# Gate rows and evictions ahead of the sums' splits, one output-weight tile per half step, the weight tile first in each step's transfers

## The chip, the cores and the metric

One Trainium2 chip, one core of it. A core has TensorE (PE, the matrix engine, with a granted clock of 1.2 or 2.4 GHz), VectorE (DVE), ScalarE (ACT), GpSimd (POOL) and SyncE (SP, which here only issues transfers). Each runs its own instructions in program order; semaphores hold them together. The metric is device time of one execution in microseconds (us); lower is better.

## The reference

One layer of a hybrid encoder trunk on x of 1024 tokens by 1024 features, all float32. What matters here:

```python
h = rmsnorm(x, norm1_g)
z = h @ w_in + b_in                     # 1024 x 2312
aq, ak, av, mq, mk, mv, mo, mi, mf = split(z)
att = window_sink_attention(aq, ak, av, sinks)        # 16 chunks of 64 tokens
ml = sigmoid(mo) * mlstm_chunkwise(conv_silu(mq, mk), mv, mi, mf)
#   log_f = log_sigmoid(mf); cum_f = cumsum(log_f)    # the gate rows
x = x + concat(rmsnorm(att), rmsnorm(ml)) @ w_out
x = x + conv_ffn(rmsnorm(x))
return rmsnorm(x, final_g)
```

## The kernel before

Each float32 product is done as three passes over operands that are split in a high part (rounded, written by ACT) and a low part (the rest, written by DVE): high*high, high*low, low*high. So every weight tile and every activation passes through ACT and then DVE before PE can use it.

The work around the change is the first projection, z = h @ w_in, and what is woven into it:

- **Blocks.** `z_block(b)` computes one tile of 128 columns of z for all tokens, 48 matmuls of 128x512. Blocks 0 to 3 (0 is the gates' 8 columns) are done as the input arrives; blocks 4 to 10 follow, two PSUM buffers taking turns. Block b waits for the low part of its own weights (`z_split`, from `weight_low(b)`) and for the eviction of the block two before it (`z_scaled`, from `z_scale`, which multiplies the PSUM result by each token's 1/rms). `z_keep` on ACT then adds the bias.
- **Gate rows.** Block 0's eight rows become the mLSTM's decay rows: `gate_logs` (ACT: abs, exp, log, with two table loads), `gate_rows(0)` and `gate_rows(1)` (DVE: two scans and some elementwise work on 4 partitions), `gate_exps` (ACT). They are turned by PE between blocks 6 and 7.
- **Sums.** Part of z (columns MO and MV, the `wide_unit` calls after block 10) is computed by a scheme with seven half-size products (`WIDE_ORDER`) instead of eight. It needs sums and differences of slices of h, made on POOL (`add_sums(kk)`, four of 128x512 for each of four kk, in the order `SUM_TURN`), split by `sums_high` (ACT) and `sums_low` (DVE), stored to DRAM by `store_sums` (SP) and loaded back later (`load_sums`). It also needs sums of weights, made on POOL by `add_weights(p, q)` from the tiles that `load_quarters` and the `w_t3` loads bring.
- **Output weights.** The eight row tiles of w_out are loaded (`load_wo`), split (`wo_high` on ACT, `wo_low` on DVE) and stored (`store_wo`), at half steps given by the table `WO_AT`, in four places of SBUF given by `WO_PLACE`, a place being loaded again when `WO_FREED` says that its content is stored.
- **Attention.** From block 8 on, chunk n of the attention runs in half steps beside the blocks: `att_step(b+1, half)` gives n. In each, DVE does `att_top(n)`, ACT `att_exps(n)`, DVE `att_sum(n)`, POOL `att_p_scale(n)`, PE turns and attends.
- **The order on each engine is written out by hand.** ACT and DVE run a loop over blocks b and halves, each with a fixed list of calls; POOL a loop over chunks n with the tables `weight_sums` and `DECAY_KEEPS`; SP a loop over n, the number of the weight tile, whose body lists the transfers of that step in the order in which they are issued. SP stops at each wait, and all transfers behind it stop too.

In the profile, L2350 is the blocks' matmuls, L1595 and L1600 are `z_scale`, L1561 `weight_low`, L1810 `sums_low`, L1633 to L1651 the gate rows, L1155 `sums_high`, L1146 `sum_scale`, L1011 `weight_high`, L1742 and L1125 the output weights' split, L925 to L931 `add_sums`, L949 `add_weights`, L2584 to L2588 the wide units. At the end of the stage, `ml_key` (L1139) scales the turned keys for PE's `ml_state` (L2485), and `wide_gate` (L1130) is the sigmoid of the output gate.

## Time and profile before

| | us |
|---|---|
| median of 3 runs | 1010.95 (1010.78 to 1011.40) |
| the profiled execution's own time | 1012.26 |
| its span, first to last instruction | 1010.5 |
| PE busy in it | 981.3 (97%) |
| DVE, ACT, POOL busy | 763.8, 527.9, 96.4 |
| mean granted TensorE clock | 0.991 of 2.4 GHz |

The table is read from the first part of the page: PE is busy for all but 29.2 us of the span, and no other engine for more than 76% of it. The list of waits and the chain that ended last say where the 29.2 us are.

### The profile page before, as it was taken

The page shows a single profiled execution, that of the slowest core. Times are in us where ns is not written, and L with a number is a line of the kernel's source. Part 1 is how long each engine was busy: PE and PEld are TensorE (multiplying, and loading weights), DVE is VectorE, ACT ScalarE, POOL GpSimd, SP SyncE. Part 2 cuts the span into 40 slices and gives each one's busy share as a digit, 9 for nine tenths or more (in the row PEclk, how much of TensorE's full clock was granted, in tenths as well). Part 3 has the DMA queues.
Part 4 walks back from the last instruction along what each step waited for, and adds up shares of the span by engine and source line. Part 5 has one row for each costly group of instructions (what it writes and reads, how often), then busy time and mean ns, then how long its engine had stood idle before and what let it go on. Part 6 is the DMA issues. An engine that isn't in the chain of part 4 may idle for free.

```text
span 1010.5 us, 12942 instructions
## 1 busy us (share of the span) xinstructions
PE 981.3 (97%) x4665; PEld 802.7 (79%) x4665; DVE 763.8 (76%) x1166; ACT 527.9 (52%) x1020; POOL 96.4 (10%) x77
## 2 busy tenths in 40 slices
PE   8968989999999999999999999999999999999997
PEld 6746877787788888888888888888888888888886
DVE  4377577887755668997777777877776879995796
ACT  4875454667853326654544544544543634444574
POOL 2380133342310000000000000000000000000000
PEclk9998999999999999999999999999999999999999
DMA  9465968717622242333223223223322999035104
GB/s 340 166 229 193 395 225 289 256 58 228 211 84 84 84 146 63 113 97 111 77 70 99 82 65 100 87 63 96 92 63 84 392 350 359 1 113 190 42 1 166
DMA packets 101239, 150.67 MB, mean 149 GB/s; under 512 B 6572, under 2 KB 56876, under 8 KB 100152
## 3 DMA queue, kind: packets, MB, share of 16 engines
q1 hardware_dynamic: 100360, 149.24, 43.6%
q8 instruction: 37, 0.61, 0.2%
q10 hardware_dynamic: 720, 0.61, 0.2%
q0 software_dynamic: 96, 0.00, 0.1%
q14 instruction: 26, 0.21, 0.1%
HBM read 112.62 MB, written 36.74 MB: 148 GB/s over the span
## 4 chain that ended last, share of the span: by engine, by line
PE 85%; DVE 5%; DMA 3%; ACT 3%; SPq 2%; POOL 1%; issue 1%; DVEq 0%; ACTq 0%
PE pz L2653 8%; PE pz L2654 8%; PE pz L2655 8%; PE pd L2653 6%; PE pd L2654 6%; PE pd L2655 6%; PE pz L2350 5%; PE pd L2679 4%; PE pd L2678 4%; PE pd L2676 4%; PE pz L2679 3%; PE pz L2678 3%; PE pz L2676 3%; PE pd L2544 3%; PE pd L2546 3%; PE pd L2545 3%
## 5 line engine op out<-in xcount | busy, mean ns | idle before, releaser
L1349 ACT ACTIVATE ws_hi<-raw 128x512 fp32r<-128x512 f32 x88 | 52.9, 626 | 102.8 <-PE pz L2655 47.3
L2653 PE MATMUL pz<-ht_hi,ws_hi 128*128 128x512 f32 x240 | 93.5, 390 | 0.0
L2655 PE MATMUL pz<-ht_hi,ws_lo 128*128 128x512 f32 x240 | 93.4, 389 | 0.0
L2654 PE MATMUL pz<-ht_lo,ws_hi 128*128 128x512 f32 x240 | 93.4, 389 | 0.0
L2653 PE MATMUL pd<-ht_hi,ws_hi 128*128 128x512 f32 x200 | 77.9, 390 | 0.0
L2655 PE MATMUL pd<-ht_hi,ws_lo 128*128 128x512 f32 x200 | 77.8, 389 | 0.0
L2654 PE MATMUL pd<-ht_lo,ws_hi 128*128 128x512 f32 x200 | 77.8, 389 | 0.0
L2097 DVE SCALAR_TENSOR_TENSOR gate<-u,vec,gate 128x1023 f32<-128x1023 f32 (+1 forms) x44 | 56.5, 1283 | 19.4 <-ACT gate L1391 18.6
L2067 DVE TENSOR_TENSOR ws_lo<-raw,ws_hi 128x512 fp32r<-128x512 f32 x88 | 58.5, 686 | 0.7 <-ACT ws_hi L1349 0.7
L2097 DVE SCALAR_TENSOR_TENSOR lift<-u,vec,lift 128x1023 f32<-128x1023 f32 (+1 forms) x44 | 56.2, 1278 | 0.1
L1424 ACT ACTIVATE d_hi<-a 128x512 fp32r<-128x512 f32 x44 | 27.8, 631 | 54.2 <-PE pd L2679 26.3
L2653 PEld LDWEIGHTS pz<-ht_hi,ws_hi 128*128 128x128 f32 x240 | 45.0, 188 | 10.0 <-issue 0.7
L2655 PEld LDWEIGHTS pz<-ht_hi,ws_lo 128*128 128x128 f32 x240 | 45.0, 188 | 9.5
L2654 PEld LDWEIGHTS pz<-ht_lo,ws_hi 128*128 128x128 f32 x240 | 45.0, 188 | 9.2
L2584 PE MATMUL pz<-w_hi,h_hi 128*128 128x512 f32 x112 | 45.8, 409 | 5.9 <-DVE z L1600 2.6
L2676 PE MATMUL pz<-d_hi,d_hi 128*128 128x512 f32 x132 | 51.4, 389 | 0.0
L2678 PE MATMUL pz<-d_lo,d_hi 128*128 128x512 f32 x132 | 51.4, 389 | 0.0
L2679 PE MATMUL pz<-d_hi,d_lo 128*128 128x512 f32 x132 | 51.4, 389 | 0.0
L2678 PE MATMUL pd<-d_lo,d_hi 128*128 128x512 f32 x132 | 51.3, 389 | 0.0
L2679 PE MATMUL pd<-d_hi,d_lo 128*128 128x512 f32 x132 | 51.3, 389 | 0.0
L2676 PE MATMUL pd<-d_hi,d_hi 128*128 128x512 f32 x132 | 51.3, 389 | 0.0
L2544 PE MATMUL pd<-wo_hi,mix_hi 128*128 128x512 f32 x128 | 50.7, 396 | 0.0
(339 smaller groups left out, 2602.8 us busy)
## 6 DMA issues: line engine op xcount, KB each, us to landing
raw<-in_w_up SPq DMA_DIRECT2D x48, 512.0 KB, 5.1
b<-in_w_down SPq DMA_DIRECT2D x49, 256.0 KB, 7.1
act_rows<-gate SPq DMA_DIRECT2D x22, 512.0 KB, 2.6
a<-act_rows SPq DMA_DIRECT2D x44, 256.0 KB, 4.7
x_in<-in_x SPq DMA_DIRECT2D x8, 512.0 KB, 12.1
s_hi_rows<-s_hi SPq DMA_DIRECT2D x4, 1024.0 KB, 3.9
s_lo_rows<-s_lo SPq DMA_DIRECT2D x4, 1024.0 KB, 6.9
wo_hi_rows<-wo_new_hi SPq DMA_DIRECT2D x8, 512.0 KB, 4.3
```

The costliest lines, as they stand in the source:

```text
L1349: nc.scalar.activation(ws_hi[m][:, :, :], summand(p, i), ACT.Copy).then_inc(s["ws_hi_made"], 1)
L2067: nc.vector.tensor_tensor(ws_lo[m][:, :, :], summand(p, i), ws_hi[m][:, :, :].bitcast(F32), ALU.subtract)\
L2097: nc.vector.scalar_tensor_tensor(out=dst[:, back:], in0=src[:, 0:S - back], scalar=w, in1=dst[:, back:], op0=ALU.mult, op1=ALU.add).then_i ...
L2350: ins = mm(dst[:, h * HALF:(h + 1) * HALF], w[:, c], h_part(part, k, h), start=first, stop=last)
L2544: mm(bank[4 + n % 4], mix_hi[u][:, k, :], wo_hi[:, k, c], start=k == 0, stop=False)
L2584: mm(wide_bank(t), h_hi[:, k, tok], hi[:, kk, :], start=begins and q + kk == 0, stop=False, skip_group_check=not begins)
L2653: mm(dst, wh[:, k, :], xh[:, k, :], start=begins and k == 0, stop=False, skip_group_check=not begins)
L2654: mm(dst, wh[:, k, :], xl[:, k, :], start=False, stop=False, skip_group_check=not begins)
L2655: ins = mm(dst, wl[:, k, :], xh[:, k, :], start=False, stop=k == KH - 1, skip_group_check=not begins)
L2676: mm(dst, d_hi[m, 0][:, c], d_hi[m, 1][:, :], start=begins and k == 0, stop=False, skip_group_check=not begins)
L2678: mm(dst, d_hi[m, 0][:, c], d_lo[m, 1][:, :], start=False, stop=False, skip_group_check=not begins)
L2679: ins = mm(dst, d_lo[m, 0][:, c], d_hi[m, 1][:, :], start=False, stop=k == KT - 1, skip_group_check=not begins)
```

## The change

Nothing is computed otherwise; instructions and transfers change their places. On PE the order is the same, word for word.

1. **ACT**: `gate_logs` right behind `z_keep(0)`, ahead of `sums_high(1)`; `sums_high(2)` behind `sum_scale(3)`; `sums_high(0)` behind `weight_high(6)`.
2. **DVE**: `z_scale(1)`, `z_scale(2)`, `z_scale(3)` and `gate_rows(0)` ahead of all `sums_low`; these stand at the second half of b = 3 (kk 1), 4 (kk 2) and 5 (kk 0 and 3). In the wide units `weight_low` stands behind `att_keep`.
3. **WO_AT**: at most one output-weight tile in each half step, from (6, 0) to (10, 0) instead of from (5, 0) to (9, 1). The last tile takes another place.
4. **SP**: the weight tile first in each step, the sums' stores and output-weight transfers behind it; `load_quarters` a step later; `load_sums(5)` and the bias rows ahead of the last output-weight store and of the `w_t3` loads; `spread_decay` a step later.
5. **POOL**: the weight sums one or two chunks later; the decay's masks (`DECAY_KEEPS`) and ACT's exponentials (`DECAYS`) one chunk later at first.
6. **ACT, end of the stage**: `ml_key(1)` ahead of four `wide_gate`.

```diff
-DECAYS = {12: (0,), 13: (1,), 14: (2,), 15: (3, 4), 16: (5, 6, 7)}
-DECAY_KEEPS = {11: (0,), 12: (1, 2), 13: (3, 4), 14: (5, 6), 15: (7,)}
+DECAYS = {13: (0,), 14: (1, 2), 15: (3, 4), 16: (5, 6, 7)}
+DECAY_KEEPS = {12: (0,), 13: (1, 2), 14: (3, 4), 15: (5, 6, 7)}
-WO_AT = {(5, 0): 0, (5, 1): 1, (6, 1): 2, (7, 0): 3, (7, 1): 4, (8, 1): 5, (9, 0): 6, (9, 1): 7}
+WO_AT = {(6, 0): 0, (6, 1): 1, (7, 0): 2, (7, 1): 3, (8, 0): 4, (8, 1): 5, (9, 0): 6, (10, 0): 7}
-WO_PLACE = (0, 1, 2, 3, 0, 1, 3, 0)
-WO_FREED = {4: 0, 5: 1, 6: 3, 7: 4}
+WO_PLACE = (0, 1, 2, 3, 0, 1, 3, 1)
+WO_FREED = {4: 0, 5: 1, 6: 3, 7: 5}
...
             def load_quarters():
                 sp.wait_ge(*sum_stored[3])
+                sp.wait_ge(wo_stored[0], 32 * 2)
...
-            store_sums(1)
-            store_sums(2)
             for n in range(7, LAST_BLOCK + 1 + UNITS):
                 if n in LOADED:
                     load_tile(n)
                 if n == 7:
-                    load_wo(0)
-                    load_wo(1)
-                    store_sums(0)
+                    store_sums(1)
                 if n == 8:
                     store_rows()
+                    load_wo(0)
+                    store_sums(2)
+                    store_sums(0)
+                if n == 9:
+                    load_wo(1)
+                    store_sums(3)
                     load_wo(2)
                     store_wo(0)
+                if n == 10:
                     load_wo(3)
                     store_wo(1)
...
                 if n == 13:
                     sp.wait_ge(s["z_done"], LAST_BLOCK + 1)
                     load_sums(5)
...
+                    store_wo(7)
+                    sp.wait_ge(wo_stored[0], 32 * (NK // 2))
+                    for q in range(2):
+                        sp.dma_start(w_t3[q][:, :], w_wide[0, 2 + q]).then_inc(b22_loaded, 16)
...
-            weight_sums = {2: (5, 0), 3: (5, 1), 6: (6, 0), 7: (6, 1), 8: (7, 0), 9: (7, 1)}
+            weight_sums = {4: (5, 0), 5: (5, 1), 7: (6, 0), 8: (6, 1), 9: (7, 0), 10: (7, 1)}
...
-            sums_high(1)
-            z_keep(0)
-            sums_high(2)
-            gate_logs()
+            z_keep(0)
+            gate_logs()
+            sums_high(1)
             sum_scale(3)
-            sums_high(0)
+            sums_high(2)
...
             att_total_keep()
+            ml_key(1)
             for i in range(NT // 2, NT):
                 wide_gate(i)
...
             z_scale(0)
-            sums_low(1)
             z_scale(1)
             z_scale(2)
-            sums_low(2)
...
-                    if (b, half) in ((3, 1), (5, 0)):
-                        sums_low(0 if b == 3 else 3)
+                    if half == 1 and b in (3, 4, 5):
+                        for kk in {3: (1,), 4: (2,), 5: (0, 3)}[b]:
+                            sums_low(kk)
```

DVE before, from block 0's eviction to that of block 4 (`s_lo_277` to `s_lo_280` are the sums' low parts, `zq` and `z` the evictions, `row_*` the gate rows, `w_lo_268` the low part of block 6's weights):

```order
L1810 TENSOR_TENSOR s_lo_278<-s_sum_274,s_hi_282 128x2048
L1595 TENSOR_TENSOR zq<-pz,rstd_row 128x8x64 x2
L1595 TENSOR_TENSOR zq<-pd,rstd_row 128x8x64 x2
L1810 TENSOR_TENSOR s_lo_279<-s_sum_275,s_hi_283 128x2048
L1595 TENSOR_TENSOR zq<-pd,rstd_row 128x8x64 x2
L1633 SCALAR_TENSOR_TENSOR row_b<-row_b,row_c 4x1024
L1636 SCALAR_TENSOR_TENSOR row_d<-reset,row_b 4x1024
L1637 COPY row_b<-row_d 4x1024
L1639 TENSOR_TENSOR row_a<-row_a,row_b 4x1024
L1640 COPY row_c<-row_b 4x7
L1810 TENSOR_TENSOR s_lo_277<-s_sum_273,s_hi_281 128x2048
L1561 TENSOR_TENSOR w_lo_268<-w_raw_265,w_hi_271 128x1024
```

The same place of DVE with the change (its lines are numbered some higher):

```order
L1599 TENSOR_TENSOR zq<-pz,rstd_row 128x8x64 x2
L1599 TENSOR_TENSOR zq<-pd,rstd_row 128x8x64 x4
L1637 SCALAR_TENSOR_TENSOR row_b<-row_b,row_c 4x1024
L1640 SCALAR_TENSOR_TENSOR row_d<-reset,row_b 4x1024
L1641 COPY row_b<-row_d 4x1024
L1643 TENSOR_TENSOR row_a<-row_a,row_b 4x1024
L1644 COPY row_c<-row_b 4x7
L1814 TENSOR_TENSOR s_lo_278<-s_sum_274,s_hi_282 128x2048
L1565 TENSOR_TENSOR w_lo_268<-w_raw_265,w_hi_271 128x1024
```

Two of the three low parts that stood ahead of block 6's weights are behind them now, and the gate rows' first half has nothing of the sums ahead of it.

ACT before, from the last scaled sum to the gates' logarithm (`s_hi_282` and `s_hi_283` are the high parts of kk 1 and 2):

```order
L1155 ACTIVATE s_hi_282<-s_sum_274 128x2048
L1040 ACTIVATE row_a<-row_d,gate_b 4x1024
L1042 ACTIVATE row_b<-row_d,gate_b 4x1024
L1155 ACTIVATE s_hi_283<-s_sum_275 128x2048
L1053 ACTIVATE row_c<-row_b 4x1024
L1055 ACT_TABLE_LOAD
L1055 ACTIVATE row_c<-row_c 4x1024
L1057 ACT_TABLE_LOAD
L1057 ACTIVATE row_c<-row_c,one 4x1024
```

ACT with the change, the same place:

```order
L1041 ACTIVATE row_a<-row_d,gate_b 4x1024
L1043 ACTIVATE row_b<-row_d,gate_b 4x1024
L1054 ACTIVATE row_c<-row_b 4x1024
L1056 ACT_TABLE_LOAD
L1056 ACTIVATE row_c<-row_c 4x1024
L1058 ACT_TABLE_LOAD
L1058 ACTIVATE row_c<-row_c,one 4x1024
L1156 ACTIVATE s_hi_282<-s_sum_274 128x2048
```

Both high parts, each of which waits for POOL's sums, are behind the logarithm now.

SP before, the transfers around the end of block 10 (`w_t_0_291`, `w_t_1_292` are the `w_t3` tiles):

```order
L619 DMA wo_hi_rows<-wo_new_hi_61 128x1024
L619 DMA wo_lo_rows<-wo_new_lo_57 128x1024
L681 DMA w_t_0_291<-in_w_wide 128x1024
L681 DMA w_t_1_292<-in_w_wide 128x1024
L594 DMA h_hi<-s_hi_rows 128x4x512
L594 DMA h_lo<-s_lo_rows 128x4x512
L687 DMA bias_rows<-in_b_in 128x512 x2
```

SP with the change:

```order
L595 DMA h_hi<-s_hi_rows 128x4x512
L595 DMA h_lo<-s_lo_rows 128x4x512
L684 DMA bias_rows<-in_b_in 128x512 x2
L620 DMA wo_hi_rows<-wo_new_hi_62 128x1024
L620 DMA wo_lo_rows<-wo_new_lo_58 128x1024
L689 DMA w_t_0_291<-in_w_wide 128x1024
L689 DMA w_t_1_292<-in_w_wide 128x1024
```

The bias rows no longer stand behind the last output-weight store and the two weight tiles.

## Rows read from the trace of the kernel before

**Rows 1.** The page: length of the profiled execution.
```profile
span 1010.5 us, 12942 instructions
```
**Rows 2.** Waits of PE: who waited for whom, us in total, times, longest.
```profile
PE pz L2350 <- DVE zq L1595: 13.1, 2, 12.2
PE pz L2584 <- DVE z L1600: 2.6, 1, 2.6
PE pz L2584 <- DVE ml_v L1782: 1.6, 1, 1.6
PE pd L2485 <- ACT ml_k L1139: 1.2, 1, 1.2
PE pd L2413 <- ACT probs_t L1111: 0.7, 1, 0.7
```
**Rows 3.** Timeline of PE, 79 us: start, us, instruction, in brackets idle before it.
```profile
79.38 1.19 PE L2350 MATMUL pz<-h_hi,w_hi 128*128 128x512 f32 x2 [12.17 <-DVE zq L1595]
```
**Rows 4.** The chain that ended last, blocks 6 and 7: start, us.
```profile
79.38 13.71 PE pz L2350 x48
...
94.74 11.11 PE pz L2350 x48
```
**Rows 5.** Timeline of DVE, 54 to 83 us.
```profile
54.61 1.29 DVE L1595 TENSOR_TENSOR zq<-pz,rstd_row 128x512 f32<-128x512 f32 x2
...
64.99 1.22 DVE L1633 SCALAR_TENSOR_TENSOR row_b<-row_b,row_c 4x1024 f32<-4x1024 f32 x1 [1.93 <-ACT row_c L1057]
...
68.55 1.58 DVE L1637 COPY row_b<-row_d 4x1024 f32<-4x1024 f32 x1
70.17 2.18 DVE L1639 TENSOR_TENSOR row_a<-row_a,row_b 4x1024 f32<-4x1024 f32 x1
...
73.54 2.29 DVE L1810 TENSOR_TENSOR s_lo<-s_sum,s_hi 128x2048 fp32r<-128x2048 f32 x1
75.75 2.28 DVE L1561 TENSOR_TENSOR w_lo<-w_raw,w_hi 128x1024 fp32r<-128x1024 f32 x1
...
81.66 1.21 DVE L1647 TENSOR_TENSOR row_c<-m_prev,row_d 4x1024 f32<-4x1024 f32 x1
```
**Rows 6.** Timeline of POOL, 49 to 56 us.
```profile
49.76 1.30 POOL L925 TENSOR_TENSOR s_sum<-s_sum 128x512 f32<-128x512 f32 x1
...
52.51 3.20 POOL L929 TENSOR_TENSOR s_sum<-s_sum 128x512 f32<-128x512 f32 x1
```
**Rows 7.** Timeline of ACT, 45 to 60 us.
```profile
45.30 1.14 ACT L1146 ACTIVATE s_sum<-x_turned,vec 128x1024 f32<-128x1024 f32 x1
...
51.66 1.13 ACT L1040 ACTIVATE row_a<-row_d,gate_b 4x1024 f32<-4x1024 f32 x1
...
59.06 1.06 ACT L1053 ACTIVATE row_c<-row_b 4x1024 f32<-4x1024 f32 x1
```
**Rows 8.** Busy time by window, each engine; then granted clock, DMA share, GB/s.
```profile
79.38:82.00 2.62, 2.62 (x6) 2.12 (x7) 2.55 (x3) 2.32 (x2) 0.00 (x0) 0.50 1.03 338
...
152.30:157.00 4.70, 4.70 (x15) 3.70 (x16) 2.47 (x4) 1.84 (x6) 1.99 (x1) 0.64 0.97 320
```
**Rows 9.** Timeline of DVE, 131 us.
```profile
131.27 3.42 DVE L1668 SCALAR_TENSOR_TENSOR qk_acc<-z,vec,qk_acc 128x1022 f32<-128x1022 f32 x1
```
**Rows 10.** The chain that ended last, 140 to 165 us.
```profile
140.27 2.54 DVE wo_new_lo L1742
...
154.07 10.15 DMA bias_rows<-in_b_in
```
**Rows 11.** The page, transfers: KB each, median us to landing.
```profile
s_lo_rows<-s_lo SPq DMA_DIRECT2D x4, 1024.0 KB, 6.9
```
**Rows 12.** Timeline of ACT, 254 to 261 us.
```profile
254.34 2.17 ACT L1130 ACTIVATE ml_gate<-ml_gate 128x512 f32<-128x512 f32 x4
...
258.03 0.91 ACT L1139 ACTIVATE ml_k<-pd,decay 128x64 f32<-128x64 f32 x4
260.06 0.93 ACT L1139 ACTIVATE ml_k<-pd,decay 128x64 f32<-128x64 f32 x4 [1.12 <-PE pd L2473]
```

More of the change, by code:

```diff
@@ L648, in _ @@
                 if n == 7:
-                    load_wo(0)
-                    load_wo(1)
-                    store_sums(0)
+                    store_sums(1)
                 if n == 8:
                     store_rows()
+                    load_wo(0)
[4 more added lines that the diff above has]
+                    store_sums(3)
                     load_wo(2)
                     store_wo(0)
+                if n == 10:
                     load_wo(3)
                     store_wo(1)
-                if n == 9:
-                    store_sums(3)
+                    load_wo(4)
                     store_wo(2)
-                    load_wo(4)
-                if n == 10:
-                    store_wo(3)
-                    load_wo(5)
-                    load_quarters()
-                    store_wo(4)
                 if n == 11:
@@ L672, in _ @@
                           .then_inc(s["att_v_moved"], 16)
+                    load_wo(5)
+                    store_wo(3)
                     load_wo(6)
+                    store_wo(4)
+                    load_quarters()
+                if n == 12:
                     store_wo(5)
                     load_wo(7)
-                if n == 12:
                     store_wo(6)
-                    store_wo(7)
-                    sp.wait_ge(wo_stored[0], 32 * (NK // 2))
-                    for q in range(2):
-                        sp.dma_start(w_t3[q][:, :], w_wide[0, 2 + q]).then_inc(b22_loaded, 16)
                 if n == 13:
@@ L694, in _ @@
                     weights_used(sp, 16)
+                    spread_decay()
                     load_sums(7)
-                if n == 18:
-                    spread_decay()
                 if n == 23:
@@ L957, in _ @@
                     add_weights(*weight_sums[n])
+                if n == NC - 1:
+                    add_weights(4, 0)
                 for i in DECAY_KEEPS.get(n, ()):
                     decay_keep(i)
-            add_weights(4, 0)
             add_weights(4, 1)
@@ L1185, in _ @@
                         att_exps(n)
+                    if (b, half) == (4, 0):
+                        sums_high(0)
                     if half == 0 and b <= LAST_BLOCK:
@@ L1257, in _ @@
             for i in range(NT - 1):
-                ml_key(i + 1)
+                if i:
+                    ml_key(i + 1)
                 if i == NT - 3:
@@ L1764, in wide_keep @@
                     dve.wait_ge(s["gates_t_ready"], 1)
-                    dve.wait_ge(wo_stored[1], 32 * (NK // 2))
+                    dve.wait_ge(wo_stored[0], 32 * (NK // 2))
                 if m == 24:
@@ L1832, in _ @@
                         weight_low(b + 2)
-                    if 0 <= v < UNITS - 1:
-                        weight_low(LAST_BLOCK + 2 + v)
                     if half == 0 and b < LAST_BLOCK:
@@ L1841, in _ @@
                                 att_keep(m)
+                    if 0 <= v < UNITS - 1:
+                        weight_low(LAST_BLOCK + 2 + v)
                     if 0 <= n < NC:
```

## The prediction

> **What bounds the kernel now.** Read first the list of waits of PE, since PE is busy for nearly the whole span. Two waits of the blocks' matmuls for an eviction make 13.1 us, one of them 12.2; later there are single waits of 2.6, 1.6, 1.2 and 0.7 us [rows 2]. Then PE's timeline: block 6 starts at 79.38 after 12.17 us of idleness, so block 5 had ended at 67.21 [rows 3]; the other wait, 0.9, is block 5's own start. The chain that ended last shows block 6 taking 13.71 us, where block 7 takes 11.11 [rows 4], and the windows show why: from 79.38 to 82.00 the granted clock was 0.50 of 2.4 GHz, that is 1.2 GHz [rows 8].
>
> What held block 6 is on DVE [rows 5]. It needs the low part of its weights (w_lo at 75.75, till 78.03) and the eviction of block 4 (z_scale, till 79.2). Both stand behind the gate rows, which start at 64.99 when ACT's logarithm ends, and behind a sums' low part at 73.54. The gates' logarithm on ACT was late because the gates' bias starts only at 51.66, behind the first high part of the sums, and the abs only at 59.06, behind the second; ACT's last scaled sum had ended at 46.4 [rows 7]. Between them ACT waited for POOL's sums.
>
> **The first stall, walked anew.** ACT: the bias pair follows the scaled sums at 46.4; it takes 2.3 (two instructions, the first 1.13), and from the abs's start to the logarithm's end the trace has 64.95 - 59.06 = 5.9 [rows 5, 7]. So the gate rows start at 46.4 + 2.3 + 5.9 + 0.2 for the hand-overs = 54.8 instead of 65.0. The evictions of blocks 1 to 3 are done by then: three of 1.2 to 1.3 us [rows 5] from 46.5 on.
>
> The gate rows now meet POOL's sums, which run without a break. An add on POOL takes 1.30 alone, and 3.20 when it meets DVE [rows 6]; a copy takes 1.58 and a product of the two row tiles 2.18 on DVE where POOL is busy, against 1.21 for the same form at 81.66 with POOL idle [rows 5]. In the rows the two take strict turns: each waits for the other's instruction to end. The eviction from PSUM at 54.61 took 1.29 though POOL was in its slow add [rows 5, 6], so evictions don't take part.
>
> By the Trainium skill (GPSIMD Engine Reference, section 1, Specifications), GpSimd shares its SBUF interfaces with VectorE and contends with DVE instructions that have two SBUF inputs. The trace agrees, by the 2.18 against 1.21 for a form with two; this speaks against a change that moves such rows into POOL's busiest stretch, and it is priced below from the rows.
>
> With turns, DVE goes: waits 0.4 for POOL, 1.1, scan 2.3 (66.2 to 68.5 in the trace) after 1.1, copy 0.6 after 1.1, subtraction 1.1 after 1.1, the small copy 0.1 after 1.1: the first half of the gate rows ends at 64.9. That is 10.1 us where the trace before has 8.5 (64.99 to 73.5). Then the low part of kk 1, 2.3 (at 73.54) to 67.2; block 6's low weights 2.2 (at 75.75) to 69.4; block 4's eviction 1.2 to 70.6. ACT is ahead: the high part of kk 1 (1.9), the scaled sums of kk 3, the high part of kk 2, three biases and block 6's high weights end at 64.9. Block 6 starts at 70.8 instead of 79.4. Block 5 starts 0.9 earlier, since its bank is free at once, and ends at 66.1. The wait is 4.7 instead of 12.2.
>
> Bounds: without any turns lost to POOL (five of about 1.1) DVE is ready at 67.4 (ACT's high weights, 64.9, then bound the low ones), a wait of 1.3; with POOL first at one place more, and one in the evictions, 73, a wait of 7. I take 4.7, since the turns at 68.55 to 75.75 are the nearest rows.
>
> Clock: it fell to 1.2 GHz after the wait of 12.17 us and cost 13.71 - 11.11 = 2.6 us. It fell also after the wait of 2.6 us, where a window of 4.7 us had 0.64 [rows 8], a loss of 0.36 x 4.7 = 1.7. So after 4.7 us of idleness I expect it to fall and take the middle, 2.1. Block 6 ends at 70.8 + 11.1 + 2.1 = 84.0, before at 93.1: **9.1 us** won.
>
> The Trainium skill (TensorE: Matmul & The Clock Gate, Part 1) says that the throttled clock is the default and activity releases it; the trace agrees at both waits. By the page alone one could also hope for a full clock behind a short wait, which would make the sum 2.1 better; that is the second rival.
>
> **What is late next.** Block 7 starts behind the turning of the gate rows (1.6 us) at 85.6. It needs block 5's eviction, which now has behind it on DVE the second half of the gate rows (about 7.5 with two turns lost), the low part of kk 2 (2.3), the low weights (1.2) and itself (1.2): 70.6 + 12.2 = 82.8, and some 84 if ACT, which must do two exponentials, a table load, the high part of kk 3 and block 7's high weights, is the slower. A margin of 1.5 us, so nothing is charged.
>
> Then the output weights. Their tile 1 is loaded only after the sums of kk 2 are stored (split at about 80.4, a transfer lands 6.9 after its issue [rows 11]: 87.5), behind the stores of kk 0 in SP's row: issued at 88.6, here by about 97. ACT stands in `wo_high(1)` until then, and the high weights of block 9 and the attention's values are queued behind it; PE wants the latter at 102.9 and gets them at about 102.3. This is the thinnest margin of the change (0.6), and cost nothing by my sum; each us that the transfer is later is a us of PE.
>
> **The waits of the attention stage.** The 2.6 us wait and the 0.7 before it come from a late DVE: the tap at 131.27 took 3.42 and the output-weight low part at 140.27 took 2.54, both beside POOL's weight sums [rows 9, 10], where a form of this size with POOL idle takes 1.21 [rows 5], and two output-weight tiles stand in the half steps just ahead of block 10's eviction. The change puts those weight sums one to two chunks later and has one tile fewer there. That frees 2.2 + 1.2 + 1.3 = 4.7 us of DVE ahead of an eviction that was 2.6 late. So 2.6 goes, with the clock's 1.7 behind it, and 0.7: **5.0 us**. The 1.6 us wait [rows 2] is for the bias rows: their transfer starts at 154.07, behind a store and two weight tiles in SP's row, and takes 10.15 [rows 10]. Now it is issued with block 10's end and lands at least 4 us earlier relative to PE: **1.6 us**.
>
> **Edits at nothing.** The weight sums, the quarters (issued at about 120 and needed by POOL at 137), the decay transfers and the later masks have several us of room each. They cost up to 2 if the room is used up. `ml_key(1)` ahead of four sigmoids takes away the wait of 1.2 [rows 2]: it would run some 2 us earlier than 258.03. But the sigmoids, the table load and the root, 3.7 us from 254.34 on, then stand between it and the next `ml_key` (260.06, with 1.12 of idleness ahead of it [rows 12]), which becomes up to 1 us late, and PE waits there: net 0.2, bounds 0 and 1.2. I charge 0.
>
> **The sum.** 9.1 + 5.0 + 1.6 = 15.7. The span goes from 1010.5 [rows 1] to 994.8. What lies around the span was 1.8 us (1012.26 less 1010.5), and this execution stands 1.3 above the median; taken off the median, 1010.95 - 15.7 = 995.2 us. Behind 260 us nothing is touched and PE is bound by itself, so what is won there stays.
>
> **The rivals.**
> *The attention stage keeps its waits.* The first stall shrinks, but POOL's weight sums meet DVE elsewhere, or the output weights' loads come late, so that 4 to 6 us of the second and third term are not seen, or new waits take their place: 995.2 + 5 = 1000. For it: DVE is full there, and PE, with no stalls to wait in, gives it less time. Against: the sums of DVE's work per half step stay below PE's.
> *The first stall nearly goes.* DVE gets through with few turns lost, the wait is 1.3, the clock stays up: 4.7 - 1.3 + 2.1 = 5.5 better, 989.7. But then block 7's eviction is the next late thing and takes back 1 or 2: 991.
> *The transfers stop the queue; slower than before.* SP is one row, and load_wo, store_wo and the sums' stores of 1 MB each wait for one another there. If each of output-weight tiles 1 to 3 comes a whole store (6.9, rows 11) later than ACT stands at it, ACT holds the weights and values of blocks 8 to 10: 3 x 6.9 = 20.7 lost, less 15.7: 1016. It decides from 16 us of such lateness on. Against: before the change PE's list has no wait for an output weight or for what stands behind one [rows 2], with the same eight loads and stores in a like weave. One late transfer costs some us only, which is the first rival.
> *The change doesn't take effect* where the logarithm is late for another reason (the gates' row transfer, or the bias's semaphores): the first term falls to about 4, 1000; it lies with the first rival.
>
> **How the numbers follow.** The forecast's case (993 to 998) 60%; the first rival and its like (998 to 1003) 23%; the second (988 to 993) 12%; the slower side 2%; something between 1003 and 1013, 3%. Two runs of this kernel can be told apart by about 0.2%, 2 us. Faster by more than that 0.95, the same 0.03, slower 0.02. The range that leaves at most 2 in 10 out is 990.5 to 1001.5, which holds the clock's and the turns' bounds and half of the first rival.
>
> **What would show it.** PE's wait before block 6 near 4.7 us, between 66 and 71; gate rows starting on DVE at 54.8, with copy and subtraction again at 1.6 and 2.2; a granted clock of 0.5 behind it; block 7 from about 85.6 without a wait; no wait of wide units for block 10's eviction nor for ml_v; PE's first matmul of the output projection some 16 us before the old one. Wrong would be: gate rows later than 57; a wait of PE for the attention's values or for ACT's high weights of block 9; new waits of more than 1 us between 100 and 250.

## The result, and the profile after

The changed kernel takes 1002.79 us (median; 1002.39 to 1003.63, 4 runs), the kernel before 1010.98 (1010.78 to 1011.4, 4 runs): ratio 0.992, with a 95% interval of 0.9902 to 0.9937. That is 8.2 us less, where 15.7 were forecast, and 1.3 us above the forecast range. Its profiled execution has a span of 1000.7 us, 9.8 less than before's [rows 1]; before's profiled run stood 1.3 above its own median and this one 0.3 below its own, so the two numbers agree.

The waits of PE in the changed kernel (who waited for whom, us in total, times, longest), against [rows 2]:

```profile
PE pz L2353 <- DVE zq L1599: 5.6, 1, 5.6
PE pd L2416 <- ACT probs_t L1112: 2.3, 1, 2.3
PE pz L2587 <- DVE ml_gate L1786: 1.6, 2, 1.1
...
PE pz L2587 <- DVE ml_v L1786: 1.2, 1, 1.2
PE pd L2488 <- ACT ml_k L1140: 1.0, 1, 1.0
PE pd L2403 <- ACT sink_e L1095: 0.6, 1, 0.6
PE pz L2587 <- DVE z L1604: 0.4, 1, 0.4
```

Two words for what follows: PE *turns* a tile when it transposes it by a matmul with the identity (`pd<-ident,...`), and `sink_e` is the last exponential of a chunk of the attention; PE writes the scores of a later chunk only behind it. The 12.2 has become 5.6, the 2.6 has become 0.4, and the 0.7 for probabilities at 140 us is gone. Two are new: 0.6 for `sink_e` and 2.3 for the transposed probabilities, both in a stretch where PE had not waited before. PE's timeline places them (start, us, instruction, idle before it):

```profile
70.75 1.19 PE L2353 MATMUL pz<-h_hi,w_hi 128*128 128x512 f32 x2 [5.55 <-DVE zq L1599]
...
115.94 1.16 PE L2403 MATMUL pd<-z,zq 64*128 64x128 f32 x16 [0.59 <-ACT sink_e L1095]
119.37 1.09 PE L2416 MATMUL pd<-ident,probs 128*128 128x128 f32 x4 [2.27 <-ACT probs_t L1112]
144.08 0.50 PE L2587 MATMUL pz<-w_hi,h_hi 128*128 128x512 f32 x1 [0.37 <-DVE z L1604]
```

Windows behind the first and the third of these, in the columns of [rows 8] (start:end, length, busy time of PE, of PE's weight loads, of DVE, ACT and POOL, each with its instructions; then granted clock as a share of 2.4 GHz, DMA share, GB/s):

```profile
70.75:74.50 3.75, 3.75 (x9) 2.98 (x10) 3.68 (x3) 2.32 (x2) 3.12 (x1) 0.51 0.97 315
119.40:122.40 3.00, 3.00 (x10) 2.58 (x11) 2.85 (x6) 0.05 (x1) 0.00 (x0) 0.53 0.96 351
```

So the clock was at 1.2 GHz behind both. Following one point of the work through both traces gives the balance. Block 7 starts at 94.74 before [rows 4] and at 85.20 after, 9.5 earlier. The first probabilities are turned at 124.22 and 114.75: still 9.5. The next turning is at 137.26 and 132.09: 5.2 earlier, so 4.3 us were lost between, which is 0.6 and 2.3 of waiting and 1.4 of slow clock. At 156.72 and 146.95 it is 9.8 again, since the 2.6 us wait and its slow clock are gone; from there to the end it stays between 9.6 and 9.9, but for the waits for a key at 259 and 252 us.

A caution on sizes below. PE's start-up, untouched by any of these kernels, waited for up to 1.8 us in the executions profiled here, and the wait for the first value rows came out as 1.23 and 2.62 us in two kernels that do the same up to there. Positions are therefore compared from block 7 on, and a median says nothing below 1 us.

### The profile page after: what moved, and what is told of

Its sections match the earlier page's. It is cut to its first block, busy times and chain, and to the rows that moved or that the text cites. A ratio compares the mean times of both kernels' runs of the same rounds, so it can differ in the third digit from the quotient of the medians.

```text
span 1000.7 us, 12943 instructions
## 1 busy us (share of the span) xinstructions
PE 980.1 (98%) x4665; PEld 802.2 (80%) x4665; DVE 768.1 (77%) x1166; ACT 528.1 (53%) x1020; POOL 95.5 (10%) x77
## 4 chain that ended last, share of the span: by engine, by line
PE 80%; DMA 9%; DVE 5%; SPq 3%; ACT 2%; issue 1%; DVEq 0%; ACTq 0%
PE pz L2656 8%; PE pz L2658 8%; PE pz L2657 8%; PE pd L2656 6%; PE pd L2658 6%; PE pd L2657 6%; PE pd L2679 4%; PE pd L2681 4%; PE pd L2682 4%; DMA wo_lo_rows<-wo_new_lo 3%; PE pz L2679 3%; PE pz L2681 3%; PE pz L2682 3%; PE pd L2547 3%; PE pd L2549 3%; PE pd L2548 3%
## 5 line engine op out<-in xcount | busy, mean ns | idle before, releaser
L2549 PE MATMUL pd<-wo_hi,mix_lo 128*128 128x512 f32 x128 | 50.0, 390 | 0.0
```

The source lines that it names most:

```text
L2549: ins = mm(bank[4 + n % 4], mix_lo[u][:, k, :], wo_hi[:, k, c], start=False, stop=k == NK - 1)
```

## What stood behind the new wait

ACT's timeline in the changed kernel, the high parts of output-weight tiles 1 to 4 and the first transposed probabilities:

```profile
97.16 1.15 ACT L1126 ACTIVATE wo_new_hi<-wo_raw,vec 128x1024 fp32r<-128x1024 f32 x1 [5.50 <-DMA wo_raw<-in_w_out]
...
103.76 1.15 ACT L1126 ACTIVATE wo_new_hi<-wo_raw,vec 128x1024 fp32r<-128x1024 f32 x1 [0.60 <-DMA wo_raw<-in_w_out]
...
110.01 1.15 ACT L1126 ACTIVATE wo_new_hi<-wo_raw,vec 128x1024 fp32r<-128x1024 f32 x1 [1.57 <-DMA wo_raw<-in_w_out]
...
117.62 1.13 ACT L1126 ACTIVATE wo_new_hi<-wo_raw,vec 128x1024 fp32r<-128x1024 f32 x1
118.66 0.57 ACT L1112 ACTIVATE probs_t<-pd 64x512 f32<-64x512 f32 x1
```

Three tiles in a row come late. Tile 1's lateness is the chain that the forecast had walked (store of the sums kk 2, load, eviction):

```profile
79.86 8.25 DMA s_lo_rows<-s_lo
...
89.06 8.08 DMA wo_raw<-in_w_out
...
97.16 1.16 ACT wo_new_hi L1126
```

It was forecast here "by about 97", and PE did not wait for the attention's values. The harm came one stage later, from tile 3. `load_wo(3)` waits until ACT has evicted tile 1 (`wo_hi_made`), so it was issued at 98.34, right at the end of ACT's 97.16 row: tile 1's lateness was handed on. ACT has tile 3 at 110.01, DVE's `wo_low(3)` follows at 111.19, and `att_top(1)` stands behind that in DVE's row (113.12), though its scores had long been there; so the exponentials of chunk 1, block 8's bias, `wo_high(4)` and the first transposed probabilities (118.66) are each late. The transfers in that stretch, by windows of 84 to 120 us of before and of after:

```profile
84.00:120.00 36.00, 36.00 (x184) 29.57 (x184) 19.92 (x33) 17.90 (x25) 0.61 (x1) 0.99 0.74 277
```

```profile
84.00:120.00 36.00, 33.14 (x183) 27.38 (x182) 20.08 (x35) 16.20 (x32) 1.65 (x2) 0.98 1.02 355
```

The queue is full: a DMA share of 1.02 where it was 0.74. Before, the sums' stores of 2 MB each were issued at 54.6, 61.9, 75.9 and 99.9 us, and output tiles 0 and 1 were loaded from 63.7 on. Now three of these stores, 6 MB, go out between 79.5 and 91.5 us, and output tiles 0, 1 and 2 are loaded from 77.4, 88.1 and 91.7 on, in the stage in which the weights of blocks 9 and 10 are loaded.

## The experiments

Fourteen kernels: e1 to e4, e11 and e12 change one thing each, with what hangs on it; the others put together what these had shown. All medians are of five rounds (key undone: three), each beside the kernel before on the same chip (1010.7 to 1011.2).

| run | us, median | ratio to before, 95% |
|---|---|---|
| tile 1 in a free place (e1) | 1002.51 | 0.9908 to 0.9935 |
| bias rows first (e2) | 1002.15 | 0.9902 to 0.9929 |
| GpSimd's sums later (e3) | 1003.17 | 0.9908 to 0.9933 |
| order of gate rows undone (e4) | 1008.31 | 0.9965 to 0.9986 |
| GpSimd's sums and splits later (e5) | 1006.68 | 0.9946 to 0.9971 |
| queue by need (e6) | 1000.35 | 0.9881 to 0.9908 |
| e6, tiles 4 to 6 later (e7) | 999.75 | 0.9874 to 0.9904 |
| all together (e8) | 998.49 | 0.9864 to 0.9891 |
| e8, sums' load first again (e9) | 999.31 | 0.9873 to 0.99 |
| e9 without GpSimd's part (e10) | 999.35 | 0.9872 to 0.9902 |
| tiles 4 to 6 later alone (e11) | 1002.66 | 0.9907 to 0.9932 |
| key of chunk 1 undone (e12) | 1003.45 | 0.9911 to 0.9938 |
| e9, wait for its own store (e13) | 998.97 | 0.9859 to 0.9892 |
| e10, wait for its own store (e14) | 999.69 | 0.9869 to 0.9898 |

### The order of the gate rows undone (e4)

```diff
-            z_keep(0)
-            gate_logs()
             sums_high(1)
+            z_keep(0)
+            sums_high(2)
+            gate_logs()
```

(with `sums_low` back at their old places on DVE.)

> The changed kernel, with one part undone: the order of the gate rows, the evictions and the sums' splits on ScalarE and VectorE as before; the turn of SyncE's queue, the output weights' half steps and the weight sums stay as changed. Theory A (the forecast's first term: the gate rows' place is worth 9 us and nothing else in the change is): TensorE's wait ahead of block 6 is back at about 12 us with its drop of the clock, block 7 starts at 94 to 95 us, and the time is 1009 to 1012, less up to 3 us if the later output weights still spare the attention stage its waits there. Rival B (part of the 9 us comes from SyncE's turn, the weight tile first): the wait stays below 9 us.

The wait is back at 11.94 and the kernel is 5.5 us slower than the changed one (1008.31):

```profile
78.76 0.76 PE L2353 MATMUL pz<-h_hi,w_hi 128*128 128x512 f32 x1 [11.94 <-DVE zq L1598]
```

Theory A holds (1008.31 is in its range of 1009 to 1012, less up to 3), rival B falls. It also has a wait of 2.10 at 126.3 for the transposed probabilities: 7 us later than in the changed kernel, with the stage itself. The new wait therefore belongs to the queue and the output weights, not to PE being earlier.

### Output-weight tile 1 in a free place (e1)

```diff
-WO_PLACE = (0, 1, 2, 3, 0, 1, 3, 1)
+WO_PLACE = (0, 2, 1, 3, 0, 1, 3, 1)
@@ SyncE, n == 8
                     load_wo(0)
+                    load_wo(1)
                     store_sums(2)
```

(Tile 2 takes tile 1's old place and its wait for the store of kk 2.)

> The changed kernel, with output-weight tiles 1 and 2 in each other's places: tile 1's place is free early, so its load is issued right behind tile 0's (about 79 us) and no longer behind the second store of the sums (88.1 us). In the changed kernel ScalarE then stood 5.5 us for that tile, and TensorE waited 0.6 us at 116 and 2.3 us at 119 us, with a drop of the clock behind it (4.3 us in all). Theory A (tile 1 comes late, and all that is queued behind its eviction is late with it): ScalarE's 5.5 us wait goes, the waits at 116 and 119 us go with the drop, and the time falls by 3.5 to 4.5 us, to about 998.5. Rival B (the order alone: the eviction of tile 4 now stands ahead of the first transposed probabilities): the 2.3 us wait stays within 0.5 us and the time stays within 1 us of 1002.8. Rival C (the transfers as a whole are too many there): tile 1's wait goes but tiles 2 and 3 come late instead, with 1 to 3 us for each, and less than half of the 4.3 us is won.

Theory A's time falls here. ACT's 5.5 us wait for tile 1 is gone, but it stands as long for the next thing, the tile of block 9's weights, and tile 3 is late again:

```profile
97.97 1.06 ACT L1014 ACTIVATE w_hi<-w_raw 128x1024 fp32r<-128x1024 f32 x1 [5.40 <-DMA w_raw<-in_w_tiles]
...
109.88 1.15 ACT L1128 ACTIVATE wo_new_hi<-wo_raw,vec 128x1024 fp32r<-128x1024 f32 x1 [2.70 <-DMA wo_raw<-in_w_out]
```

PE still waits 1.78 us there, and the time does not move. That is rival C: several transfers are late behind one another. Block 9's weights were issued at 86.20, behind 4 MB of stores issued from 79.8 on. Tile 3 was issued at 97.81, hardly earlier than in the changed kernel, for another reason: its load now stood in SP's row behind that of weight tile 10 (97.43), which waits until PE is through with block 7. Yet tile 1's place had its share: from the turning of the attention's values behind block 7 to the turning of probabilities at about 131 us, e1 takes 33.4 us (97.24 to 130.63) and the changed kernel 35.9 (96.22 to 132.09), since the wait is 1.1 shorter and the clock behind it stayed at 1.00. So 2.5 of the 4.3 us are won there, more than half; 1.5 of them go again in longer waits at 144 (1.32) and 157 us (1.77).

### The queue by need (e6), and tiles 4 to 6 later (e7, e11)

```diff
                 if n == 9:
-                    load_wo(1)
-                    store_sums(3)
+                    store_sums(0)
                     load_wo(2)
                     store_wo(0)
-                if n == 10:
                     load_wo(3)
+                    store_sums(3)
+                if n == 10:
                     store_wo(1)
```

(shown against the changed kernel; e1's edit is in it too. The store of kk 0 goes from ahead of block 9's weight tile to behind it, the load of tile 3 from behind block 10's weight tile to ahead of it, and at n == 11 the store of tile 3 ahead of the load of tile 5.)

> The changed kernel with SyncE's queue put by need: tile 1 in a free place and loaded right behind tile 0; the store of sum 0 (2 MB) behind the load of weight tile 9 and not ahead of it; the load of output-weight tile 3 ahead of weight tile 10's; stores behind loads. With tile 1's place alone ScalarE's 5.5 us wait had only passed to weight tile 9 (issued 86.2, used 97.97), and the time had not moved. Theory A (what lands late in 84 to 120 us stands behind stores in one queue that is full; the order decides): weight tile 9 is used by 94 us, output tile 3 by 108 us, and TensorE's wait for the first transposed probabilities falls to 0.3 to 1.2 us, without a drop of the clock: 999 to 1001. Rival B (the sum of the bytes decides, any order): another transfer is late by as much and the time stays within 1 us of 1002.5.

Theory A holds in the time, in tile 3 and in PE's wait; weight tile 9 was used at 96.77, not by 94, but held by PE and by no transfer. The same bytes move, but tile 3 is issued at 94.21 and evicted at 106.32, and PE has no wait from 71 to 130.9 us; the window shows it, PE busy for all of its 36 us with the DMA share as high as before:

```profile
84.00:120.00 36.00, 36.00 (x201) 29.84 (x201) 22.87 (x39) 17.22 (x38) 1.66 (x2) 1.00 1.02 389
```

Two things changed at once here, and no run takes them apart: the stores went behind the loads, and tile 3's load no longer stands behind the wait for block 7. Tile 3 took 11.7 and 12.1 us from its issue to ACT's use in the changed kernel and in e1, where ACT stood for it, and it had at most 12.1 here; a faster landing is not shown, an issue 3.6 us earlier than e1's is.

The time is 1000.35, 2.4 us less than the changed kernel. By the positions all of the 4.3 us are won by the turning at 128.08 (31.6 us behind the turning of the values at 96.51, where the changed kernel takes 35.9). Most of it is lost at 132.75, where PE waits 1.82 us, again for transposed probabilities, with a granted clock of 0.51 behind it.

e7 adds, and e11 does alone:

```diff
-WO_AT = {(6, 0): 0, (6, 1): 1, (7, 0): 2, (7, 1): 3, (8, 0): 4, (8, 1): 5, (9, 0): 6, (10, 0): 7}
+WO_AT = {(6, 0): 0, (6, 1): 1, (7, 0): 2, (7, 1): 3, (8, 1): 4, (9, 0): 5, (9, 1): 6, (10, 0): 7}
```

> The same queue as in the run above, and output-weight tiles 4, 5 and 6 one half step later on ScalarE and VectorE, so that the eviction of tile 4 stands behind the first transposed probabilities and not ahead of them. Theory A (that eviction's 1.05 us is part of the wait, what is left after the loads): TensorE's wait there goes to 0 to 0.3 us and the time is 0.5 to 1.2 us below the run above. Rival B (the tiles' loads alone): no difference over 0.3 us, or slower where the later tiles hold VectorE.

The wait that goes in e7 is this one at 132.75, not the one at 119, which was gone already. PE then waits 2.06 us for block 10's eviction at 143.2 instead: 999.75, no difference that the runs can tell. That eviction stands behind a DVE row of 128x1024 (the `qk_acc` TENSOR_SCALAR at 138.08) that took 2.89 us beside POOL's weight sum of 3.38; with POOL idle it takes 0.80 (before, 149.23). The same row takes 2.89 in e10, e13 and e14, which have waits of 2.06, 1.75 and 2.06 there.

> The changed kernel with output-weight tiles 4, 5 and 6 one half step later, and nothing else. The eviction of tile 4 (1.05 us on ScalarE) then stands behind the first transposed probabilities. Theory A (tile 3's late transfer and the row on VectorE behind it make most of the wait at 119 us, the eviction the rest): TensorE's wait of 2.3 us falls by 1.0 us to about 1.2, perhaps without the drop of the clock, and the time falls by 0.5 to 2.5 us. Rival B (the order alone made the wait): it goes altogether, with 3 to 4 us.

In the old queue, PE's waits are 0.36 and 1.83 (now for POOL's scaling of the probabilities) in place of 0.59 and 2.27, and 1.74 and 2.02 follow at 144 and 158; the time stays (1002.66). Rival B falls; theory A's wait of about 1.2 us did not come either. The clock stayed at 1.00 behind the 1.83, so this stretch is 2.0 us shorter by the positions (97.24 to 131.13), and the two later waits take it back. The eviction of tile 4 was not the cause of the wait.

### GpSimd's last sums later (e3, e5)

```diff
+                if kk == 0:
+                    pool.wait_ge(s["z_scaled"], 5)
```

(at the head of GpSimd's sum kk; ACT's `sums_high(0)` and `(3)` a half step later.)

> The changed kernel, with GpSimd's last two sums (8 additions, which stood at 54.1 to 73.9 us) held back until VectorE has scaled the projection block that TensorE's 5.6 us wait at 65 us is for; ScalarE's copies of these sums one half step later. Theory A (VectorE's gate rows and copies take twice as long beside GpSimd's additions: the scan 3.3 against 2.3 us, the copy 1.6 against 0.6): VectorE's walk of 54.6 to 70.6 us shortens by 4 to 6 us, TensorE's wait falls to 0.5 to 1.5 us, its clock does not drop behind it (2 us more), and block 6 ends 6 to 8 us earlier; some of it may be lost to what comes next. 996 to 999 us. Rival B (the walk is set by VectorE's and ScalarE's own rows, the doubling belongs to the instructions): the wait stays above 4 us and the time stays within 1 us of 1002.8. Rival C (the late sums hold ScalarE, the stores and the output weights): the early gain is given back between 85 and 125 us.

Theory A is confirmed in DVE's rows and in PE's wait, not in the time (996 to 999); rival B falls. DVE's rows in e3, with POOL idle, and the same rows in the changed kernel, beside its additions:

```profile
56.06 2.28 DVE L1642 TENSOR_TENSOR_SCAN row_d<-reset,row_b 4x1024 f32<-4x1024 f32 x1
58.37 0.68 DVE L1643 COPY row_b<-row_d 4x1024 f32<-4x1024 f32 x1
59.09 1.21 DVE L1645 TENSOR_TENSOR row_a<-row_a,row_b 4x1024 f32<-4x1024 f32 x1
60.34 0.16 DVE L1646 COPY row_c<-row_b 4x7 f32<-4x7 f32 x1
```

```profile
56.54 3.28 DVE L1640 TENSOR_TENSOR_SCAN row_d<-reset,row_b 4x1024 f32<-4x1024 f32 x1
59.85 1.61 DVE L1641 COPY row_b<-row_d 4x1024 f32<-4x1024 f32 x1
61.49 2.20 DVE L1643 TENSOR_TENSOR row_a<-row_a,row_b 4x1024 f32<-4x1024 f32 x1
63.73 1.15 DVE L1644 COPY row_c<-row_b 4x7 f32<-4x7 f32 x1
```

Each row loses 0.9 to 1.0 us to a turn of POOL, the seven-element copy too. Without them PE does not wait ahead of block 6 at all and the clock stays at 2.4 GHz. Yet the kernel is no faster (1003.17). What was won is lost at once, much as rival C has it, though what PE waits for is DVE and no transfer:

```profile
82.40 1.19 PE L2355 MATMUL pz<-h_hi,w_hi 128*128 128x512 f32 x2 [2.35 <-DVE z L1606]
97.53 0.74 PE L2391 MATMUL pd<-ident,z 128*128 128x128 f32 x5 [2.40 <-DVE gates_t L1693]
```

e5 holds back the splits on DVE too:

```diff
+SUMS_LOW = {(3, 1): 1, (5, 0): 2, (5, 1): 0, (6, 1): 3}
```

> The changed kernel with GpSimd's last two sums held back as in the run before (which took away all of TensorE's 5.6 us wait at 65 us but gave it back at 80 and 95 us, where VectorE's scalings stood behind the late splits), and now the splits of sums 2, 0 and 3 a half step later too, behind the scalings, and the store of sum 3 behind the first store of an output-weight tile. Theory A (from 77 to 120 us the transfers set the pace, so work that TensorE does earlier only waits later): block 7 starts 5 to 7 us earlier than in the changed kernel, and the first transposed probabilities still come at 117 to 119 us; the waits around them grow, and the time is 1000.5 to 1003. Rival B (the two small waits at 80 and 95 us were all that took the gain back): the time is 995 to 998.

Neither is right. The wait at 80 us is gone, the one at 92 stays (2.55), and the kernel is 3.9 us slower than the changed one. The store of sum 3, now split later, held SyncE's queue until 101.15; block 10's weights and output tile 3 came behind it:

```profile
102.95 2.72 SPq L611 DMA_DIRECT2D wo_raw<-in_w_out  x2
```

```profile
119.25 2.08 PE L2403 MATMUL pd<-z,zq 64*128 64x128 f32 x16 [6.03 <-ACT sink_e L1098]
122.68 1.08 PE L2416 MATMUL pd<-ident,probs 128*128 128x128 f32 x4 [1.35 <-ACT probs_t L1115]
```

It was meant for another question, but it bears on the new wait. Tile 3 issued at 94.21 (e6), 97.81 (e1), 98.34 (changed) and 102.95 us (e5): PE waited 0, 1.78, 2.86 and 7.38 us for `sink_e` and the transposed probabilities together. The time of issue does not set the wait alone: e2, e11 and e12, with tile 3 at 98.7 to 99.0, have 2.2 to 2.6, but e3, at 98.73, has 0.83, its PE turning the values 1.3 us later (97.53) than the changed kernel's (96.22).

### The bias rows first (e2)

```diff
-                    load_sums(5)
                     sp.wait_ge(s["z_scaled"], LAST_BLOCK + 1)
...
+                    load_sums(5)
```

> The changed kernel, with the two loads of the bias rows issued ahead of the two loads of the sums of pair 5 on SyncE's queue, so at about 144.1 us instead of 145.8. Theory A (they come late because 2 MB of sums stand ahead of them in the same queue): they land at about 148 instead of 156, VectorE's 1.3 us wait goes, and the wait of TensorE for the wide values (1.2 us) goes: 1.0 to 1.4 us faster than the changed kernel, about 1001.5. Rival B (their landing time is set by all transfers under way, not by the two ahead): they land after 153 us, and less than 0.4 us is won.

The bias rows land 4.6 and 6.7 us after their issue at 144.58 instead of 9.48, and PE's wait for the value rows is gone, as theory A has it. In its place PE waits 0.73 us for the sums that now stand behind them:

```profile
156.93 0.47 PE L2587 MATMUL pz<-w_hi,h_hi 128*128 128x512 f32 x1 [0.73 <-DMA h_lo<-s_lo_rows]
```

By the positions in the trace it wins 1.3 us over the changed kernel; the median (1002.15) is 0.6 below it, which the runs cannot tell from nothing.

### The key of chunk 1 undone (e12)

```diff
-            ml_key(1)
             for i in range(NT // 2, NT):
                 wide_gate(i)
...
-                if i:
-                    ml_key(i + 1)
+                ml_key(i + 1)
```

> The changed kernel with the key of chunk 1 on ScalarE behind the gates' sigmoids again, as before the change. The forecast put the move at 0.2 us net: TensorE's wait for the key at the first state is back (1.2 us), the one at the second state (1.0 us) goes, and the time stays within 0.5 us of the changed kernel. Rival (both waits stay): 1 us slower.

PE waits 1.20 us at the first state (251.32) and no longer at the second; in the changed kernel it is the other way about, with 1.03:

```profile
252.19 0.66 PE L2488 MATMUL pd<-ml_v,ml_k 128*64 128x129 f32 x8 [1.03 <-ACT ml_k L1140]
```

So 0.17 net, where 0.2 was forecast and 0 charged. The median is 0.7 above the changed kernel, beyond the 0.5 that was expected, but less than the runs can tell; in this run's trace the wait for the value rows, which the edit does not touch, is 2.62.

### All together, and what the end of the stage waits for (e8, e9, e10, e13, e14)

e8 is e7 with e2's order of the bias rows and e5's order on POOL, ACT and DVE.

> All together: the run above (queue by need, tiles 4 to 6 later), GpSimd's last sums and the splits later, and the bias rows ahead of the sums of pair 5. Theory A (the waits are those of the gate rows beside GpSimd, 7 us with the clock; of the first probabilities, 4.3; of the bias rows, 1.2): up to 12 us less than the changed kernel, of which I expect 6 to 9: 994 to 997. Rival B (the transfers of 77 to 150 us take back what is won ahead of them): 998.5 to 1001.

998.49 us: the fastest kernel here, 1.9 us below e6 and 4.3 below the changed one, and still above theory A's range (994 to 997), at the lower edge of rival B's (998.5). Its largest wait is 3.3 us at 150.7. e9 puts the load of the sums of pair 5 ahead of the bias rows again and both ahead of the store of tile 6, and `sums_high(3)` behind `wo_high(0)`; e10 is e9 with POOL, ACT and DVE as in the changed kernel, apart from the output tiles.

> The best run so far with three things moved: the loads of the sums of pair 5 first again, the bias rows behind them, but both now ahead of the store of output-weight tile 6 (with the bias rows first, TensorE had waited 3.3 us at 150.7 us, which the profile puts down to VectorE's last value rows; the load of the sums had been issued 3 us later than it could be); and ScalarE's copy of sum 3 behind the eviction of output tile 0, since it had held the gates' way to TensorE (wait 2.6 us at 91 us). Theory A (in both places one long item stood ahead of a needed one): the wait at 91 us falls to 0.5 to 1.5, the one at 151 us to 0.5 to 1.5, and the time is 995 to 996.5. Rival B (the full queue of 77 to 150 us sets the end of the stage): both fall but others take their place, and the time stays within 0.7 of 998.5.

> The run above with GpSimd's sums and the splits as in the changed kernel, so only SyncE's queue and output tiles 4 to 6 differ from that. Theory A (TensorE's 5.6 us wait beside GpSimd's additions is worth its time to the end, once the transfers keep up): 2 to 4 us slower than the run above. Rival B (what is won ahead of 77 us is lost in the transfers): within 0.7 us of it. Against the run with tiles 4 to 6 later (999.75): the earlier load of the sums and of the bias rows gives 0.3 to 1 us.

The wait at 91 us is gone in e9, but 1.64 comes at 114.4, and 3.44 stays at 150; the time (999.31) is above both of e9's ranges, nearest to rival B's. Both kernels take the same time, so e10's rival B holds, and e10 has no wait at 150. DVE's row in e9 names what it stood for, a store:

```profile
152.67 0.75 DVE L1789 SCALAR_TENSOR_TENSOR ml_v<-pz,rstd_tok,bias_rows 128x512 f32<-128x512 f32 x1 [3.48 <-DMA wo_lo_rows<-wo_new_lo]
```

The first value row waits until every even tile's store has landed, tile 6's too, though it only takes tile 4's place.

```diff
-                    dve.wait_ge(wo_stored[0], 32 * (NK // 2))
+                    dve.wait_ge(wo_stored[0], 32 * 3)
```

> The run with queue and GpSimd changed (999.3), where VectorE's first value row stood 3.5 us until 152.67 for the second store of output-weight tile 6 (issued 141.3) and TensorE 3.4 us behind it. The first value row writes where tile 4 was, so it now waits for tile 4's store alone. Theory A (a wait on more stores than the row needs takes back what the earlier stages won): VectorE's row starts when the bias rows land, about 149.4 us, TensorE's wait falls to 0 to 0.6 us, and the time is 995.5 to 997. Rival B (the sums of pair 5, issued 139.2 at the tail of the same queue, land as late as the store): TensorE waits until 151 to 153 for them, and at most 1 us is won.

> The same single wait changed in the run with the queue alone (999.35), where VectorE stood 0.5 us for that store and TensorE did not wait. Theory A (the 3 us that GpSimd's later sums win ahead of 80 us reach the end once that wait is gone): no more than 0.5 us faster than 999.35, so 2 to 3.5 us slower than its neighbour. Rival B: both within 1 us of each other.

In e13 the wait falls from 3.44 to 0.41 as expected, but 2.09 at 115.8 (POOL's scaling of the probabilities, with a slow clock behind it) and 1.75 at 142 (block 10's eviction) have grown, and the time is 998.97: theory A's wait came, its time (995.5 to 997) did not, and no more was won than rival B allowed. What is ahead of both waits is no transfer but DVE and POOL in each other's way: POOL's scaling took 1.99 there (113.72) and 1.04 in the next chunk, DVE's `qk_acc` row 2.89 beside the weight sum. Against e14, GpSimd's part is worth 0.7 us, not 3. So rival B of e14 holds. Why e8 and e13 end so near one another with different waits is not settled.

## Why the forecast was wrong, point by point

1. **The first stall (9.1 us): right, to 0.4.** Gate rows started at 54.60 (forecast 54.8), their first half ended at 64.9 (64.9), block 6 started at 70.75 (70.8), block 7 at 85.20 (85.6). The wait was 5.55, not 4.7, since block 5 ended at 65.20, 0.9 before the forecast's 66.1, in part by a shorter start-up. The copy and the product took 1.61 and 2.20 in place of [rows 5]'s 1.58 and 2.18. e4 gives it back in the main: block 6 starts 8.0 us later than in the changed kernel, and the median is 5.5 higher.
2. **Block 7's eviction: right.** It ended on DVE at 82.8 (forecast 82.8 to 84), and PE did not wait.
3. **The output weights ("cost nothing by my sum"): this step failed, by 4.3 us.** Tile 1 came at 97.14, as forecast, and the values were in time. The failure is that only this tile was walked. Its store, taken at 6.9 us from [rows 11], the page's median over the trace before, took 8.25, and began 0.5 us earlier than forecast; its load took the 8 us that it was given. But nothing was said of tiles 2 and 3, which stand behind it in SP's row: tile 3's load waits for tile 1's eviction and for PE's end of block 7. It went out at 98.34 and was used at 110.01, and DVE's row carried this to `att_top(1)`. The forecast's own sign of being wrong, a new wait of more than 1 us between 100 and 250, shows it (2.27); the sign that it named for this path, a wait for the attention's values, does not. e5 and e6 show it from both sides: 7.4 us with that load 4.6 us later, none with it 4.1 us earlier, though each moves other transfers too. e1 shows that tile 1 alone was not the cause, as I had believed on reading the result, though it was part of it.
4. **The attention stage (5.0 us): right in kind, 4.6 by the positions** (5.2 earlier at 132.09, 9.8 at 146.95). The wait of 2.6 came down to 0.37 and the clock held. Its sum of freed DVE time, 4.7, is not what happened in all its parts. The tap fell from 3.42 to 1.27 (126.48) and the low part from 2.54 to 1.28 (133.34), but a weight sum of POOL still stands just ahead of block 10's eviction, and a row of four elements each waited it out:

```profile
140.56 2.33 DVE L1716 TENSOR_TENSOR sink_arg<-sink,neg_top 128x4 f32<-128x4 f32 x1
142.82 1.21 DVE L1604 TENSOR_TENSOR z<-pz,rstd_row 128x1024 f32<-128x1024 f32 x1
```

   Elsewhere this row takes 0.16 (136.71). So 2.2 of the 4.7 us were lost again; the 2.5 left were just what a wait of 2.6 needed, and that the term came out right is in part luck.
5. **The bias rows (1.6 us): failed.** PE's wait is 1.23 where it was 1.6 [rows 2], at most 0.3 won. They were to land "at least 4 us earlier relative to PE". Counted from the turning at 156.72 and 146.95, they landed 7.5 us behind it before (164.22) and 9.0 behind it now (155.97): 1.5 later, not 4 earlier. They went out at 145.78, behind the load of tile 7, which stood for a store of 11.13 us until 141.6, and behind 2 MB of sums, and took 9.48:

```profile
130.49 11.13 DMA wo_lo_rows<-wo_new_lo
...
144.24 1.49 SPq L595
...
146.49 9.48 DMA bias_rows<-in_b_in
```

6. **The key: right** (0.17 by e12).

With 4.3 and 1.3 to 1.6 taken off, 15.7 becomes 9.8 to 10.1, and the profiled span gives 9.8. The medians give 8.2; the difference is the 1.3 us by which before's profiled run stood above its median and the 0.3 by which the changed kernel's stood below. The shorter start-up, 0.6 us in these two traces, is not the change's work. What happened is the first rival, "the output weights' loads come late", which had 23%. Its price was taken right (4 to 6 us). One result does not show that its chance was too low, but the sum itself had found the margin of 0.6 us on that path and looked no further along it.

## What to carry to other kernels

When work is moved past transfers, count the bytes that the move brings into each stage: here the queue was full, landing times read from the old trace were too short, and the thing to walk was not the first late tile but the last one that an in-order engine stood for, with every wait that the issuing engine meets on the way, PE's progress included. A thin margin found on one item of a series is a price for the series. With the same bytes the order of issue was worth 2.4 us (e6): loads by due time and ahead of waits they do not need, stores behind them.

## What the runs showed of the hardware

- DVE and POOL took turns in these rows, and the one that began second waited for the other's instruction to end, tiny rows too: a copy of 4x7 elements took 1.15 us beside POOL's additions and 0.16 alone, a row of 128x4 elements 2.33 beside a product of 2.40 on POOL and 0.16 alone; scan, copy and product of 4x1024 lost 1.0, 0.9 and 1.0 us each. The other way round, a scan that began 0.1 us ahead of POOL's addition took its plain 2.27 (70.53) and the addition 3.26 in place of 1.29. Evictions from PSUM (128x512) took 1.27 to 1.29 either way.
- Between 1.8 and 2.6 us the length of a wait did not decide whether the clock fell. Stretches of 2.5 to 3 us, read behind waits of 2.27 (changed kernel), 2.35 (e3), 1.82 (e6), 1.89 (e9) and 2.06 us (e10) had 0.53, 0.50, 0.51, 0.69 and 0.76; behind 2.40 (e3), 2.06 (e7), 1.83 (e11) and 1.75 us (e8, e13) they had 1.00, and so they had behind 2.62 us (e12, 158.81). Where it fell, the work up to the next fixed point took 1.2 to 1.7 us more. For one length, 2.06, both were seen:

```profile
143.20:146.00 2.80, 2.79 (x12) 2.31 (x13) 1.57 (x4) 2.80 (x8) 1.34 (x2) 1.00 1.03 414
```

```profile
140.74:143.70 2.96, 2.96 (x10) 2.39 (x11) 1.74 (x4) 2.91 (x8) 1.52 (x2) 0.76 1.04 402
```

(e7, then e10, the same place in the program.) The forecast had priced the drop from the wait's length alone.
- In the full queue the low parts of the output tiles, 512 KB each, landed 6.2 to 12.7 us after their issue, 9.9 in the median (3.6 to 10.9 before, 5.4 in the median); one of the 1 MB stores of the sums took 8.25.
